# Hybrid decoder step on one core: four edits to the load order around the attention steps

## Time and profile before

| | |
|---|---|
| median of three runs | 1985.63 us |
| the profiled execution | 1988.71 us, of which the span from first to last instruction is 1987.2 us |
| TensorE busy | 1766.7 us (89% of the span), mean granted clock 0.935 |
| VectorE, ACT, POOL busy | 58%, 41%, 16% |
| projections, attention | about 57 to 341 us, 341 to 1017 us |

### The profile page before, as it was taken

How to read it: one execution, slowest core, us unless ns; L and a number is a source line. 1 busy time by engine, 2 the same in 40 slices (tenths; PEclk the granted TensorE clock), 3 DMA queues, 4 the chain that set the end, 5 groups by cost and what they waited for, 6 DMA issues and landing times. The chain is left out here.

```text
span 1987.2 us, 28545 instructions
## 1 busy us (share of the span) xinstructions
PE 1766.7 (89%) x8894; PEld 1449.5 (73%) x8894; DVE 1160.1 (58%) x1669; ACT 815.8 (41%) x1444; POOL 313.3 (16%) x390
## 2 busy tenths in 40 slices
PE   2899999799999999989878998169999999999965
PEld 2899999688778878878756787157777777777742
DVE  5411110577768767767654332847777777777717
ACT  2332221344344434434311121226666666666623
POOL 1200000122312222222200011310000000000025
PEclk9999999799999999999867999569999999999978
DMA  6486422334423532433259334539999999999954
GB/s 205 142 252 199 132 69 62 120 99 142 143 81 120 170 93 91 145 103 99 104 186 330 120 109 181 221 114 350 400 396 399 399 397 398 399 399 397 364 191 191
DMA packets 240657, 422.91 MB, mean 213 GB/s; under 512 B 24976, under 2 KB 123168, under 8 KB 240344
## 3 DMA queue, kind: packets, MB, share of 16 engines
q1 hardware_dynamic: 187120, 321.93, 45.9%
q0 software_dynamic: 20048, 69.06, 9.7%
q10 hardware_dynamic: 33408, 30.94, 4.5%
HBM read 354.83 MB, written 78.55 MB: 218 GB/s over the span
## 5 line engine op out<-in xcount | busy, mean ns | idle before, releaser
L1787 DVE TENSOR_TENSOR wm_lo<-raw,wm_hi 128x2048 fp32r<-128x2048 f32 x156 | 352.1, 2289 | 147.6 <-ACT wm_hi L1297 147.6
L1297 ACT CAST wm_hi<-raw 128x2048 fp32r<-128x2048 f32 x160 | 301.6, 1908 | 75.4 <-PE PS L1922 75.4
L1920 PE MATMUL PS<-w_hi,hT_hl 128*128 128x512 f32 (+1 forms) x584 | 234.5, 402 | 17.7 <-issue 9.8
L1921 PE MATMUL PS<-w_lo,hT_hl 128*128 128x512 f32 (+1 forms) x584 | 228.2, 391 | 0.0
L1922 PE MATMUL PS<-w_hi,hT_hl 128*128 128x512 f32 (+1 forms) x584 | 227.8, 390 | 0.0
L1920 PE MATMUL PS<-wm_hi,xT_hi 128*128 128x512 f32 x512 | 204.1, 399 | 3.1 <-DVE xT_lo L1852 3.1
L1922 PE MATMUL PS<-wm_hi,xT_lo 128*128 128x512 f32 x512 | 201.1, 393 | 0.0
L1921 PE MATMUL PS<-wm_lo,xT_hi 128*128 128x512 f32 x512 | 200.7, 392 | 0.0
L1960 PE MATMUL PS<-xa_hi,wn 128*128 128x384 f32 x480 | 162.5, 339 | 0.2 <-ACT ev L1072 0.2
L1961 PE MATMUL PS<-xa_lo,wn 128*128 128x384 f32 x480 | 162.0, 337 | 0.0
L1962 PE MATMUL PS<-xa_hi,wn 128*128 128x384 f32 x480 | 161.8, 337 | 0.0
(11 more groups left out here) (345 smaller groups left out, 3357.9 us busy)
## 6 DMA issues: line engine op xcount, KB each, us to landing
raw<-in_w_gate SPq DMA_DIRECT2D x64, 1024.0 KB, 9.1
raw<-in_w_up SPq DMA_DIRECT2D x64, 1024.0 KB, 10.0
raw<-in_w_down SPq DMA_DIRECT2D x64, 1024.0 KB, 10.2
hT_hl<-hl_dram POOLq DMA_DIRECT2D x70, 512.0 KB, 5.5
braw<-in_w_in SPq DMA_DIRECT2D x16, 1024.0 KB, 7.2
obuf_dram<-yb ACTq DMA_DIRECT2D x32, 512.0 KB, 6.9
nd_dram<-ev ACTq DMA_DIRECT2D x72, 192.0 KB, 2.3
nd<-nd_dram SPq DMA_DIRECT2D x36, 384.0 KB, 3.6
```

What stands on the lines that cost most here:

```text
L1297: act.copy(wm_hi[:, j], raw[:, j]).then_inc(m_hi[j // 4], 1)
L1787: dve.tensor_tensor(wm_lo[:, j], raw[:, j], BF(wm_hi[:, j]), ALU.subtract).then_inc(m_lo[j // 4], 1)
L1920: pe.matmul(out, x_hi, w_hi_, start=start, stop=False)
L1921: pe.matmul(out, x_hi, w_lo_, start=False, stop=False)
```

## The change

SP's `step_load` is split into `nd_load` and `ka_load`. At a group's start the order becomes `nd` of block 0, `nd` of block 1, `ka` of block 0; from the second group on the bias loads stand between the two `nd`. Block 2 waits for the copied sample rows alone (`b_stg`). Wide piece 1 is issued one load pair later. The cache shift goes to the projection stage, between raw loads. `stageN_done` waits for less, SP waits for the stores itself, and TensorE's wait for the last copy out of PSUM moves to the first instruction that writes one of those banks. POOL copies the sample rows ahead of the product of `rr`. ACT casts piece 3 of a group ahead of `gate_in`.

```diff
@@ -537,10 +537,6 @@
     def stageN_done(eng):
 
         eng.wait_ge(n_acc, len(units))
-        eng.wait_ge(n_ev, len(units))
-        eng.wait_ge(n_wlo, 21)
-        for k in range(3):
-            eng.wait_ge(n_sto[k], 16 * (len(stores) // 3))
         eng.wait_ge(e_hl, 16 * 2 * NB)
 
     def stash_done(eng, g):
@@ -643,7 +639,11 @@
             raw_load(r)
         wide_load(0, 2)
         wide_load(0, 3)
-        for r in range(15, 21):
+        sp.dma_start(R["swa_k_sample"][0, :, 0:WIN - 1], A["cache_swa_k"][0, :, 1:WIN]).then_inc(s_shift, 16)
+        raw_load(15)
+        raw_load(16)
+        sp.dma_start(R["swa_v_sample"][0, :, 0:WIN - 1], A["cache_swa_v"][0, :, 1:WIN]).then_inc(s_shift, 16)
+        for r in range(17, 21):
             raw_load(r)
 
         def bias_loads(g):
@@ -652,50 +652,51 @@
                                                     offset=brow_dram.offset + (g * HPG + h) * (P * LROW) + 127,
                                                     ap=[[LROW - 1, P], [1, 2 * P]])).then_inc(b_bi, 16)
 
-        def step_load(g, b, s, n):
+        def nd_load(g, b, s, n):
 
             if not (isinstance(n, int) and n < 2):
                 for done in (b_sc, b_qq, b_ax, b_mn, b_vt):
                     wait_apart(sp, done, upto(n - 2))
-            if not (isinstance(b, int) and b < 2) and s == g % 2:
-                stash_done(sp, g)
-            src = nd_dram[g, ds(b, 1)].rearrange("o p n -> p (o n)")
-            sp.dma_start(nd[s][:].rearrange("p c n -> p (c n)"), src).then_inc(b_nd[s], 16)
-            if not (isinstance(n, int) and n == 0):
-                wait_apart(sp, b_sc, upto(n - 1))
+            if b == 2:
+                sp.wait_ge(b_stg, g + 1)
+            sp.dma_start(nd[s][:].rearrange("p c n -> p (c n)"), nd_dram[g, b]).then_inc(b_nd[s], 16)
+
+        def ka_load(g, b, s, n):
+
+            if n:
+                sp.wait_ge(b_sc, upto(n - 1))
             if g:
                 sp.wait_ge(b_kT, upto(g - 1))
             for half in range(2):
-                sp.dma_start(ka[s][half * HD:(half + 1) * HD, :], nd_dram[g, ds(b, 1), 0:HD, 4 * P:5 * P].rearrange("o p n -> p (o n)")).then_inc(b_kd, 16)
-
-        stageN_done(sp)
-        step_load(0, 0, 0, 0)
+                sp.dma_start(ka[s][half * HD:(half + 1) * HD, :], nd_dram[g, b, 0:HD, 4 * P:5 * P]).then_inc(b_kd, 16)
+
+        sp.wait_ge(n_acc, len(units))
+        for k in range(3):
+            sp.wait_ge(n_sto[k], 16 * (len(stores) // 3))
+        nd_load(0, 0, 0, 0)
+        nd_load(0, 1, 1, 1)
+        ka_load(0, 0, 0, 0)
         sp.dma_start(sink[:], A["sinks"][0:1, :].to_broadcast([P, HEADS])).then_inc(b_gn, 16)
         sp.dma_start(gn[:], A["gla_norm_g"][0:1, :].to_broadcast([P, DV])).then_inc(b_gn, 16)
         bias_loads(0)
         for g in range(G):
             n0 = g * NB
-            s0_, s1_ = g % 2, 1 - g % 2
-            step_load(g, 1, s1_, n0 + 1)
+            for b in range(1, NB):
+                s = (g + b) % 2
+                if b > 1:
+                    nd_load(g, b, s, n0 + b)
+                ka_load(g, b, s, n0 + b)
+                if g + 1 < G and b in (1, 7):
+                    wide_load(g + 1, 0 if b == 1 else 2)
+                if g + 1 < G and b in (2, 8):
+                    wide_load(g + 1, 1 if b == 2 else 3)
             if g + 1 < G:
-                wide_load(g + 1, 0)
-                wide_load(g + 1, 1)
-            step_load(g, 2, s0_, n0 + 2)
-            for b in range(3, 8):
-                step_load(g, b, (g + b) % 2, n0 + b)
-            if g + 1 < G:
-                wide_load(g + 1, 2)
-            step_load(g, 8, s0_, n0 + 8)
-            if g + 1 < G:
-                wide_load(g + 1, 3)
-                step_load(g + 1, 0, s1_, n0 + 9)
+                nd_load(g + 1, 0, (g + 1) % 2, n0 + 9)
                 sp.wait_ge(b_bs, upto(n0 + 8))
                 sp.wait_ge(b_bv, upto(2 * g + 1))
                 bias_loads(g + 1)
-
-        sp.dma_start(R["swa_k_sample"][0, :, 0:WIN - 1], A["cache_swa_k"][0, :, 1:WIN]).then_inc(s_shift, 16)
-        sp.dma_start(R["swa_v_sample"][0, :, 0:WIN - 1], A["cache_swa_v"][0, :, 1:WIN]).then_inc(s_shift, 16)
-
+                nd_load(g + 1, 1, g % 2, n0 + 10)
+                ka_load(g + 1, 0, (g + 1) % 2, n0 + 9)
 
         sp.wait_ge(b_gg, upto(G * NB - 1))
 
@@ -917,19 +918,20 @@
                     pool.wait_ge(b_bv, upto(2 * g))
                     pool.memset(bias[:, 1, :, 0:PAD0], NEG).then_inc(b_bv, 1)
                     pool.wait_ge(b_gn, 32)
+                if first:
+                    pool.wait_ge(b_va, upto(n))
+                    pool.wait_ge(b_nd[s], 16 * (uses + 1))
+                    pool.wait_ge(b_kd, 32 * (n + 1))
+                    pool.tensor_copy(asq[:, g], nd[s][:, 2:4, 0:NS])
+                    pool.tensor_copy(ska[:, g], ka[s][0:HD, 0:NS])
+                    pool.tensor_copy(sva[:, g], va[s][0:NS, :]).then_inc(b_stg, 1)
                 wait_apart(pool, b_rr, upto(n))
                 if first:
                     pool.wait_ge(b_rg, upto(n - 1))
                 pool.tensor_tensor(rr[:], rr[:], gn[:], ALU.mult).then_inc(b_rg, 1)
                 if first:
                     pool.wait_ge(b_rg, upto(n))
-                    pool.wait_ge(b_va, upto(n))
-                    pool.wait_ge(b_nd[s], 16 * (uses + 1))
-                    pool.wait_ge(b_kd, 32 * (n + 1))
                     pool.wait_ge(b_vrc, upto(n))
-                    pool.tensor_copy(asq[:, g], nd[s][:, 2:4, 0:NS])
-                    pool.tensor_copy(ska[:, g], ka[s][0:HD, 0:NS])
-                    pool.tensor_copy(sva[:, g], va[s][0:NS, :]).then_inc(b_stg, 1)
                     for j, t in enumerate((vr[0:NS, 0:DV], rr[0:NS, :], Rt[0:NS, 1, :])):
                         pool.dma_start(stash_dram[:, g, j], t).then_inc(b_std, 16)
                 wait_apart(pool, b_oa, upto(n))
@@ -1171,10 +1173,10 @@
             n0 = g * NB
 
             def step(n, s, uses, first, pieces=()):
+                if first and g:
+                    wide(g, 3)
                 if not (isinstance(n, int) and n == G * NB - 1):
                     gate_in(n + 1, 1 - s, uses)
-                if first and g:
-                    wide(g, 3)
                 for j in pieces:
                     if j < 2:
                         wide(g + 1, j)
@@ -2000,8 +2002,6 @@
                 if first:
                     pe.wait_ge(b_lo, upto(g * WIDE + 1))
                 wait_apart(pe, b_vrc, upto(n - 1))
-                if isinstance(n, int) and n == 0:
-                    pe.wait_ge(n_ev, len(units))
                 wide(PS[:, 2], 0).then_inc(b_vr, 1)
 
                 wait_apart(pe, b_nd[s], 16 * (uses + 1))
@@ -2016,6 +2016,8 @@
                             last = pe.matmul(PS[:, half, k0:k0 + P], nd[s][r, 2 + c, :], ka[keys][r, :], start=True, stop=True)
                 last.then_inc(b_sc, 1)
                 wait_apart(pe, b_va, upto(n - 1))
+                if isinstance(n, int) and n == 0:
+                    pe.wait_ge(n_ev, len(units))
                 pe.transpose(PS[:, 5, 0:HD], nd[s][HD:P, 4, :], ident[HD:P, HD:P]).then_inc(b_vt, 1)
 
                 wait_apart(pe, b_qq, upto(n))
```

## The result

The changed kernel took 1957.38 us (median of 4 runs, 1953.12 to 1960.17) against 1987.77 us (1983.19 to 1992.14) for the kernel before on the same chip: a ratio of 0.9857, 95% interval 0.983 to 0.9883. Its profiled execution has a span of 1958.6 us, 28.6 us less than the 1987.2 before; it is the slowest of the four runs (1960.17 us). The forecast was a gain of 44.7 us and a time of 1941; the first rival, "the block rows become the bound at the group starts", gave 33.1 and 1952.5. What happened is the first half of that rival, and more of it: it left 0.5 us of the gain in the first steps, and they lost 2.8. Its second half, 3 us in the last steps of the groups, did not come (0.3).

A forecast was written before the change was run, and what follows sets the result against it. In the attention stage TensorE is busy 624 of 676 us, so only its idle or half-clock time can go. 23.3 + 9.5 + 10.1 + 2.2 - 0.4 = 44.7 us off 1985.63 gave 1941, range 1934 to 1958.

The forecast's parts named there:

- the first rival: Group starts: late block rows leave 0.5 of 9.5 us, and last steps cost 3; gain 33.1, time 1952.5, chance 0.13.
- block 2's narrow results: Block 1 to block 2 of each group: load no longer held by stores, TensorE's gap closes; 23.3 us gained.
- piece 3 ahead of `gate_in`: First steps of groups 1 to 3: earlier cast frees the remainder, some block-row wait stays; 9.5 us gained.
- the cache shift: Step ending at block 8 of group 3 becomes a clean one, 10.1 us gained; cost in the projections 0.
- the entry: Start of the attention stage: block rows start earlier, so `gn` lands earlier; 2.2 us gained, between 1 and 3.3.
- bias and `nd` of block 1 earlier: Last step of the group before: these loads slow the block rows beside them; -0.4 us for all three, bounds 0 and -3.
- My bound: First steps of groups 1 to 3: lower bound on the piece 3 gain, near 0; upper bound 12.8 us.
- My own sign of being wrong: Projections grow by several us, block 1 keeps a gap, or gaps before the wide products exceed 2.4 us.

The follow-up runs named there:

- e5: Changed kernel, POOL issuing block rows of step n+2 in step n, but behind the three sample-row stores in a group's first step: 1939.76 us, ratio 0.9759 to the kernel before.
- e3: Changed kernel with VectorE's remainder of piece 3 split into four instructions of a quarter each: 1954.35 us.
- e4: Changed kernel with the two cache shift copies back behind the last loads of the attention stage: 1971.02 us.
- e1: Changed kernel with ACT casting weight piece 3 behind `gate_in` again: 1960.67 us.
- e6: Changed kernel with block 2's narrow results waiting again for the stores of the sample rows as well as the copies: 1959.4 us.
- e9: Changed kernel with POOL waiting again at the entry for the last stores of the projections before it starts the block rows: 1964.81 us.
- e2: Changed kernel with POOL issuing block rows of step n+2 in step n, right behind the product of `rr`: 1950.69 us, ratio 0.9816 to the kernel before.
- e10: e5 with `nd` of block 2 waiting again for the three stores of the sample rows: 1967.8 us.
- e7: e5 with piece 3 cast behind `gate_in` again and `nd` of block 1 loaded behind the keys and the bias: 1962.51 us.

## Why the prediction was wrong, point by point

| step | forecast, us | measured, us |
|---|---|---|
| block 2's narrow results | 23.3 | 22.2; block 3 gives back 1.5 |
| piece 3 ahead of `gate_in` | 9.5 | -2.8 (0.6 to -2.8 over five kernels, see below) |
| the cache shift | 10.1 | 10.1 |
| the entry | 2.2 | 2.8 |
| bias and `nd` of block 1 earlier | -0.4 | -0.3 |
| not in the forecast: block 7 to block 8 of group 1 | | -1.8 |

The measured column compares the two profiled executions, and adds up to their difference of 28.6 us within 0.1. The entry is counted from the last matmul of the projections to the transpose of the values in block 1.

**The step that failed is piece 3**, at the sentence "it needs its block rows ... and POOL's list ahead of it does not move". Up to there it was right: ACT and VectorE came as early as forecast, and there was enough to gain: 10.9 us, the first steps of the earlier trace rows less those of e5. The 12.8 of the prediction were 1.9 too many, in part because a first step keeps 0.3 to 0.5 us of idle time even in e5, which the prediction counted as loss. But POOL's list did move. The remainder reads two operands in SBUF (the on-chip memory) for 2.28 us, and in its new place it starts just ahead of POOL's product `oa`, which it shuts out until its end: 2.79 us instead of 0.73, and with it all that POOL issues behind, the block rows among it, goes out 2.05 us later (2.06 and 2.15 in groups 2 and 3). It could have been read before the run: the prediction put the remainder at 517.63, and in the kernel before `oa` starts at 517.65. The Trainium skill ("SBUF — State Buffer", section "SBUF: two separate sides") says that VectorE with two SBUF inputs and a GpSimd operation that reads SBUF take a shared port pair in turn, the whole instruction long, and that the second fully blocks. This trace agrees within 0.13 us (`oa` ends 0.60 us after the remainder, and takes 0.73 alone), and so does e3 (0.59 us after the first part). I looked at what the moved instruction waits for and who waits for it, not at what it would now run beside. Without the 2.05 us the wait in group 1 is 4.07 - 2.05 = 2.0, near the 1.8 that I had taken; in groups 2 and 3 it is 0.1 and none, where I had taken 1.2 and 0.3. So the landing times were not what failed. This is a subtraction: no run takes away the shut-out alone, since e3, which shortens it, brings a wait for VectorE.

The second part of the miss is the clock. I took the three gaps as 1.8, 1.2 and 0.3 us of plain idle time. They were 4.07, 2.19 and 2.10, 8.4 us, but the three steps are 63.0 - 49.3 = 13.7 us longer than those of e5: the other 5.3 us go with the lower clock level (means of 0.85, 0.91 and 0.91). The clock does not fall every time. In e4, which has the lists of the changed kernel in these steps, TensorE waits 2.97 us for the rows in group 1, and the window of that step is at full clock:

```profile
512.48:531.52 19.04, 15.91 (x114) 13.98 (x111) 13.65 (x29) 6.16 (x24) 13.13 (x20) 1.00 0.48 155
```

That is 2.6 us over e5's step, while group 2 of the changed kernel, which waits 2.19 us, is 3.6 over it at 0.91. So the size of the loss differs between executions of the same order. The three first steps sum to 63.0 us in the changed kernel, 61.8 in e1, 59.6 in e4, 60.3 in e6 and 62.4 in e9, against 60.2 before: from a gain of 0.6 to a loss of 2.8. My bound ("near 0 if all three wait 2.4 us and the clock falls after each") lies in there, and the 9.5 far outside. My own sign of being wrong, gaps of more than 2.4 us, came in group 1. e2 and e5 show that the block rows were the whole of it: issued early, 16.4 to 16.5 us in all three.

**Block 2** was sized rightly, and its cause is shown by e10, not by e6: while another wait held TensorE, undoing the edit cost 2.4 us. **The shift** came out as forecast on both sides (e4: 9.1 us back, and projections no shorter). In the projections the raw loads beside it land after 10.3 us (512 KB) and 9.0 (256 KB) instead of 3.6 and 6.4, and the stores after 4.7 instead of 2.5, within the slack. From the DMA issues at 220 to 245 us, first the kernel before, then the kernel after:

```profile
nraw<-in_w_in SPq DMA_DIRECT2D x3, 512.0 KB, 3.6
nd_dram<-ev ACTq DMA_DIRECT2D x6, 192.0 KB, 2.5
...
nraw<-in_w_in SPq DMA_DIRECT2D x2, 256.0 KB, 6.4
```

```profile
nraw<-in_w_in SPq DMA_DIRECT2D x3, 512.0 KB, 10.3
nd_dram<-ev ACTq DMA_DIRECT2D x6, 192.0 KB, 4.7
...
nraw<-in_w_in SPq DMA_DIRECT2D x2, 256.0 KB, 9.0
```

**The entry** is right in total but made up otherwise: `gn` is there 2.05 us earlier in the span, 1.7 us earlier counted from the last projection matmul. TensorE's first GLA product comes earlier by as much (1.7; 0.9 counted from the first wide product), and 1.1 us more come in block 0 behind it. Which edit earned it stays open (e9). **Bias and `nd` earlier** cost next to nothing: the steps into block 0 of groups 1 to 3 take 16.72, 16.73 and 16.98, before 16.72, 16.73 and 16.73.

**Not in the forecast** is the step that ends at block 8 of group 1, 18.77 instead of 16.97. TensorE waits 1.76 us there for block rows whose second half lands 9.4 us after its issue (8.0 before), beside a weight piece of 1 MB. Why the landing took longer stays open; with the same loads this step is 16.82 in e3 and 19.93 to 20.31 in e1, e4, e6 and e9, and it is 16.83 in e5, where the rows are early.

Together: 12.3 of the 16.1 us that are missing went in the first steps, and e5 gives them back. It lands at 1939.8, but that is not the forecast come true: it also gains some 3 us in steps that the forecast did not touch (17.98, 17.51 and 17.77 us before the last blocks of groups 0 to 2 become 16.82).

## What to carry to other kernels

When an instruction is moved, look at what it will run beside in its new place, not only at what it waits for: in these traces a VectorE operation with two SBUF operands held up GpSimd's product until its end, and with it every transfer in GpSimd's list behind it. Put transfers that the next step needs ahead of arithmetic in a queue's list, as long as the small stores that another engine waits for stay ahead of them. A wait that seems to cost nothing when put back may be covered by a later one; undo an edit in the version that has no other waits.

## What the runs showed of the hardware

The shut-out of POOL by VectorE, with its sizes: POOL's 128x256 product took 2.79 us beside a VectorE instruction of 2.28 us and 1.17 beside the same work in four instructions, against 0.73 alone. It works in the other direction too, in e3: 1.66 instead of 0.16 us for VectorE's 128x4 operation, which ended with POOL's 1.09 us copy; that POOL held the port from before the copy's start in the trace is argued, not shown. e7 has a second case: in group 3 the remainder starts at 827.51, 0.50 us ahead of a bias copy of 1.05 us, and takes 3.70 us instead of 2.28; it ends 2.15 us behind the copy's end. In the kernel before, the remainder fell beside POOL's bias copy too, and there the copy was the one that grew, to 1.82 us against 1.09 after; no wait in the trace ends with it. VectorE's operation is the first to start in all three, by the trace, so what decides which one is held up stays open.
